# Where the squares and sums of three norms, the clearing of semaphores and the weight sums of split units stand in a two-block layer kernel

## The reference

```
def rms_norm(x, w):
    y = xf * lax.rsqrt(jnp.mean(xf * xf, axis=-1, keepdims=True) + EPS)
    return (y * w.astype(F32)).astype(x.dtype)

def conv_ffn(h, w_up, conv_w, conv_b, w_down):
    u = causal_dwconv(h @ w_up, conv_w, conv_b)
    val, gt = jnp.split(u, 2, axis=-1)
    return (jax.nn.silu(gt) * val) @ w_down

x = x + hybrid_mixer(h, ...)          # ends in merged @ w_out
h = rms_norm(x, norm_ffn[l]);  x = x + conv_ffn(h, ...)
return rms_norm(x, norm_final)
```

## Time and profile before

| what | us |
|---|---|
| median of 3 runs | 3509.37 |
| the profiled execution | 3512.56 |
| its span, first to last instruction | 3510.7 |
| PE busy | 3206.5 (91%) |
| DVE busy | 1542.1 (44%) |
| POOL busy | 942.8 (27%) |
| ACT busy | 662.1 (19%) |

### The profile page before, as it was taken

How to read it: one execution, slowest core, us unless ns; L and a number is a source line. 1 busy time by engine, 2 the same in 40 slices (tenths; PEclk the granted TensorE clock), 3 DMA queues, 4 the chain that set the end, 5 groups by cost and what they waited for, 6 DMA issues and landing times. The chain is left out here.

```text
span 3510.7 us, 54025 instructions
## 1 busy us (share of the span) xinstructions
PE 3206.5 (91%) x22800; PEld 2145.7 (61%) x22800; DVE 1542.1 (44%) x2277; ACT 662.1 (19%) x1320; POOL 942.8 (27%) x646
## 2 busy tenths in 40 slices
PE   8998999998999798988899999999979986999998
PEld 6855856883888487647566544455758854444432
DVE  4744466225655367534788403532344334111112
ACT  2233131011111433211110001111343211000001
POOL 2201213110322345212699860000365410000000
PEclk9999999998999899999999998989999968999999
DMA  4211223220232000032345432122210013899996
GB/s 158 79 31 44 76 78 107 74 72 0 72 109 71 1 4 3 32 126 66 108 126 155 153 118 65 56 78 61 84 38 3 3 48 127 310 407 409 409 409 253
DMA packets 120558, 406.09 MB, mean 116 GB/s; under 512 B 13824, under 2 KB 18560, under 8 KB 120064
## 3 DMA queue, kind: packets, MB, share of 16 engines
q1 hardware_dynamic: 113408, 377.47, 30.7%
q0 software_dynamic: 6912, 25.17, 2.3%
HBM read 398.39 MB, written 4.19 MB: 115 GB/s over the span
## 5 line engine op out<-in xcount | busy, mean ns | idle before, releaser
L701 PE MATMUL ps<-arena 128*128 128x256 f32 x4312 | 953.1, 384 | 42.6 <-DVE arena L644 12.6
L701 PEld LDWEIGHTS ps<-arena 128*128 128x128 f32 x4312 | 828.0, 192 | 174.0 <-issue 42.7
L428 PE MATMUL ps<-arena 128*128 128x512 f32 (+2 forms) x992 | 412.3, 575 | 34.7 <-PEq L657 14.2
L428 PEld LDWEIGHTS ps<-arena 128*128 128x128 f32 (+1 forms) x992 | 190.7, 195 | 251.6 <-issue 233.6
L3306 PE MATMUL ps<-arena 128*64 128x512 f32 x1024 | 239.3, 602 | 5.1 <-PE ps L3336 2.7
L734 PE MATMUL ps<-arena 128*128 128x512 f32 x496 | 224.6, 612 | 17.2 <-DVE arena L998 17.2
L632 POOL TENSOR_TENSOR arena<-arena 128x512 f32<-128x512 f32 x66 | 93.2, 1412 | 422.9 <-POOLq L1568 104.7
L3452 POOL TENSOR_SCALAR arena<-arena,small 128x1024 f32<-128x1024 f32 x64 | 189.5, 2961 | 10.2 <-DMA arena<-in_w_mod 6.4
L811 ACT ACTIVATE arena<-ps 128x256 f32<-128x256 f32 x231 | 86.5, 383 | 550.3 <-PE ps L701 543.1
L2289 POOL TENSOR_SCALAR arena<-arena,small 128x768 f32<-128x768 f32 x32 | 70.2, 2206 | 445.2 <-DVE small L2269 445.2
L734 PEld LDWEIGHTS ps<-arena 128*128 128x128 f32 x496 | 97.3, 197 | 138.7 <-issue 133.7
(11 more groups left out here) (438 smaller groups left out, 4423.7 us busy)
## 6 DMA issues: line engine op xcount, KB each, us to landing
arena<-in_w_in SPq DMA_DIRECT2D x166, 512.0 KB, 3.7
arena<-in_w_gate SPq DMA_DIRECT2D x128, 512.0 KB, 10.9
arena<-in_w_up SPq DMA_DIRECT2D x128, 512.0 KB, 15.0
arena<-in_w_down SPq DMA_DIRECT2D x128, 512.0 KB, 9.0
arena<-in_w_mod POOLq DMA_DIRECT2D x48, 512.0 KB, 4.3
arena<-in_ffn_up SPq DMA_DIRECT2D x44, 512.0 KB, 3.8
arena<-in_w_branch SPq DMA_DIRECT2D x32, 512.0 KB, 3.7
arena<-in_w_out SPq DMA_DIRECT2D x16, 512.0 KB, 4.1
```

The lines of the kernel that those rows point to most:

```text
L428: last = nc.tensor.matmul(out[0:m, 0:j["n"]], w[:, q * m:(q + 1) * m], j["rhs"](ka + q), start=(ka + n == 0), stop=(ka + n == kt - 1))
L701: last = nc.tensor.matmul(k.bank(b)[:, 0:HT], lhs[:, q * P:(q + 1) * P], rhs[:, q, :], start=(first and q == 0), stop=(q == 3), skip_group ...
```

## The change

1. Clearing. `recycle` and its block are gone. `retire` sets the old semaphores aside, POOL clears them at the end of its list in the following output projection (`afterwards`), and `reuse_retired` gives their numbers back after it. There are two such places instead of three: the first block's output projection, and the second block's, which takes the semaphores of both former places around the delta rule.
2. Norms. `ffn_norm`, the first block's last norm and the router's norm get `early=True`. Their squares and ones-products are issued inside the projection before (`tail`): ACT squares a plane after its eviction, PE adds it after a later unit or job, and the rest behind the last unit. At the old place the inversion, root and multiplication remain. The final norm's sums stand between the last pair's scatters, which use four banks.
3. Weight sums. DVE's sums of an S unit now stand in the *unit* before it, C or S, instead of the S unit before it; where the first unit is a C, only the turn stands at the start. POOL's order becomes join of u, S1 of the next, S3 of the next.
4. Orders. The LRU projection runs its convolved tiles first and its gelu tiles last; the feed-forward up stage's last group becomes four C units, so it has ten S units; the turned inputs of the second output projection lie in other planes. (`side` in `fast_phase` has no caller in this program.)

```diff
-    def recycle(self):
-        if self.phases and self.used:
-            with self.nc.Block() as block:
-                @block.gpsimd
-                def _(pool):
-                    for s in self.used:
-                        pool.sem_clear(s)
-            self.phases.close()
+    def retire(self):
+        self.old = self.phases, self.used
         self.phases, self.used = self.ctx.enter_context(ExitStack()), []
+    def clear_retired(self, pool):
+        for s in self.old[1]:
+            pool.sem_clear(s)
+    def reuse_retired(self):
+        self.old[0].close()
...
@@ project_phase, tensor
+                if tail is not None and i >= 1:
+                    tail.add(pe, i - 1)
+            if tail is not None:
+                tail.add(pe, len(jobs) - 1)
...
@@ fast_phase, gpsimd
                     later = splits[u["s"] + 1] if u["s"] + 1 < ns else None
+                    join(pool, nc.gpsimd, u)
                     if later:
                         sum_op(pool, nc.gpsimd, later, "S1", k.st_sump)
-                    join(pool, nc.gpsimd, u)
-                    if later:
                         sum_op(pool, nc.gpsimd, later, "S3", k.st_sump)
+            if afterwards is not None:
+                afterwards(pool)
@@ fast_phase, tensor
             for ui, u in enumerate(units):
+                if tail is not None and ui >= 2:
+                    while added < units[ui - 1]["i"]:
+                        tail.add(pe, added)
+                        added += 1
...
+            if tail is not None:
+                for c in range(added, KT):
+                    tail.add(pe, c)
@@ fast_phase, scalar, at the end of finish()
+                elif tail is not None:
+                    act.wait_ge(*j["evac"])
+                    tail.square(act, i)
@@ fast_phase, vector
-            sums_early(splits[0])
-            sums_late(splits[0])
-            for u in units:
+            if units.index(splits[0]) <= 2:
+                started.add(0)
+                turn(0)
+            if units[0] is splits[0]:
+                sums_early(splits[0])
+                sums_late(splits[0])
+            for ui, u in enumerate(units):
+                later = units[ui + 1] if ui + 1 < len(units) and units[ui + 1]["kind"] == "S" else None
                 if u["kind"] == "C":
+                    if later:
+                        sums_early(later)
+                        sums_late(later)
                     finish(u, 0)
                     continue
-                later = splits[u["s"] + 1] if u["s"] + 1 < ns else None
@@ class Norm
     def act(self, act):
-        for c in range(KT):
-            self.src_in(act, c)
-            nc.scalar.activation(self.sq(c), self.src(c), ACT.Square).then_inc(self.squared, 1)
+        for c in range(0 if self.early else KT):
+            self.square(act, c)
...
     def pe(self, pe):
+        for c in range(0 if self.early else KT):
+            self.add(pe, c)
@@ experts_phase
+    sum_bank = lambda u, c: (4, 5, 0, 1)[c % 4] if u == PAIRS - 1 else 4 + c % 2
-                if c >= 2 or u >= 1:
-                    pe.wait_ge(sc_out, 8 * u + max(c - 1, 0))
+                back = 4 if u == PAIRS - 1 else 2
+                if c >= back or u >= 1:
+                    pe.wait_ge(sc_out, 8 * u + max(c - back + 1, 0))
                     for c in range(8):
                         scatter(p - 2, c)
+                        if c >= 3:
+                            norm.add(pe, c - 3)
-            norm.pe(pe)
+            for c in range(5, KT):
+                norm.add(pe, c)
@@ order
-        plan(k, project_phase, k, tiles(W_LG, 8, g, func=ACT.Gelu_apprx_tanh)
-                      + convs(W_LX, 8, xc, "lru_conv_w", "lru_conv_b", 4, nch=8),
+        plan(k, project_phase, k, convs(W_LX, 8, xc, "lru_conv_w", "lru_conv_b", 4, nch=8)
+                      + tiles(W_LG, 8, g, func=ACT.Gelu_apprx_tanh),
...
-        up = Halves(k, [u for i in range(0, 44, 4) for u in (("C", i), ("C", i + 1), ("S", i + 2, 0))], ...
+        up = Halves(k, [u for i in range(0, 40, 4) for u in (("C", i), ("C", i + 1), ("S", i + 2, 0))] + [("C", i) for i in range(40, 44)], ...
```

More of the change, by code:

```diff
@@ L322, in wtile, with project_phase @@
     return [(w[i, :, a * P:min(a + 8, kt) * P], a, min(8, kt - a)) for a in range(0, kt, 8)]
[L325 removed]
+def project_phase(k, jobs, following=(), beside=None, moves=(), ahead=None, side=None, halves=None, afterwards=None, tail=None):
     if halves is not None:
[L334 removed]
+        return fast_phase(k, jobs, halves, following, beside, moves, ahead, afterwards, tail, side)
     nc = k.nc
@@ L538, in sum_plane, with fast_phase @@
         return self.k.pl(self.sums[(4 * s + n) % len(self.sums)])
-def fast_phase(k, jobs, h, following=(), beside=None, moves=(), ahead=None):
+def fast_phase(k, jobs, h, following=(), beside=None, moves=(), ahead=None, afterwards=None, tail=None, side=None):
     nc = k.nc
@@ L576, in fast_phase @@
             j["needs_n"] = jobs[j["needs"]]["post_n"]
+    if side is not None:
+        side.begin(jobs, moved, 16 * len(moves))
     free = [(b, None) for b in range(6)]
@@ L825, in _ @@
                     finish(u, 0)
+                if side is not None:
+                    for n in range(len(js)):
+                        side.act(act, u["i"] + n)
             if late is not None:
@@ L919, in _ @@
                     sums_early(later)
+                if side is not None:
+                    side.dve(dve, u["i"] + 1)
                 dve.wait_ge(*closing(u, "P3"))
@@ L973, in act, with square, add @@
         nc = self.k.nc
-        for c in range(KT):
-            self.src_in(act, c)
-            nc.scalar.activation(self.sq(c), self.src(c), ACT.Square).then_inc(self.squared, 1)
+        for c in range(0 if self.early else KT):
+            self.square(act, c)
         act.wait_ge(self.inverse, self.base + 1)
         nc.scalar.activation(self.rt, self.inv, ACT.Sqrt).then_inc(self.root, 1)
+    def square(self, act, c):
+        self.src_in(act, c)
+        self.k.nc.scalar.activation(self.sq(c), self.src(c), ACT.Square).then_inc(self.squared, 1)
+    def add(self, pe, c):
+        pe.wait_ge(self.squared, self.base * KT + c + 1)
+        ins = self.k.nc.tensor.matmul(self.sums, self.k.const("ones"), self.sq(c), start=(c == 0), stop=(c == KT - 1), skip_group_check=True)
+        if c == KT - 1:
+            ins.then_inc(self.summed, 1)
     def src_in(self, eng, c):
@@ L983, in pe @@
     def pe(self, pe):
-        for c in range(KT):
-            pe.wait_ge(self.squared, self.base * KT + c + 1)
-            last = self.k.nc.tensor.matmul(self.sums, self.k.const("ones"), self.sq(c), start=(c == 0), stop=(c == KT - 1))
-        last.then_inc(self.summed, 1)
+        for c in range(0 if self.early else KT):
+            self.add(pe, c)
     def dve(self, dve):
@@ L3593, in order @@
                                                     [WORK + 40 + n for n in range(9)]), moves=[(pl(X + c), dr["x"][c * P:(c + 1) * P, :]) for c in range(KT)])
-        plan(k, k.recycle)
+        plan(k, k.retire)
+        ffn_norm = NormThenSilu(k, lambda c: pl(X + c), H, lambda c: k.col("norm_ffn", c), WORK + 8, early=True)
         plan(k, project_phase, k, [job(wtile(dr["w_out"], c), lambda q: pl(MRG_PL + q), "D", pl(X + c), add=pl(X + c)) for c in range(KT)],
-             halves=halved(paired(8), [MRG_PL], [WORK + 16], [WORK + 24 + n for n in range(9)]))
+             halves=halved(paired(8), [MRG_PL], [WORK + 16], [WORK + 24 + n for n in range(9)]), afterwards=k.clear_retired, tail=ffn_norm)
+        plan(k, k.reuse_retired)
         if stage == "mixed":
@@ L3611, in order, with second_block @@
                               mul=pl(hid + i), needs=len(js) - 2))
-        up = Halves(k, [u for i in range(0, 44, 4) for u in (("C", i), ("C", i + 1), ("S", i + 2, 0))], [dict(x=H_PL, t=WORK + 8)], [MRG_PL + 4 + n for n in range(4)] + [WORK + 59], [WORK + 60, WORK + 61],
+        up = Halves(k, [u for i in range(0, 40, 4) for u in (("C", i), ("C", i + 1), ("S", i + 2, 0))] + [("C", i) for i in range(40, 44)], [dict(x=H_PL, t=WORK + 8)], [MRG_PL + 4 + n for n in range(4)] + [WORK + 59], [WORK + 60, WORK + 61],
                     [WORK + 16, WORK + 17], pool=False)
         plan(k, project_phase, k, js, beside=mod_products(k, acc, range(0, 4), 2), ahead=ffn_norm, halves=up)
+        last_norm = Norm(k, lambda c: pl(X + c), lambda c: pl(X + c), lambda c: k.col("norm_final", c), WORK + 8, early=True)
         plan(k, project_phase, k, [job(wtile(dr["ffn_down"], c, FT), lambda q: pl(hid + q), "D", pl(X + c), add=pl(X + c)) for c in range(KT)],
-             beside=mod_products(k, acc, range(4, 6), 4))
-        second_block(k, dr, out, stage, X, dump, acc)
-def second_block(k, dr, out, stage, X, dump, acc):
+             beside=mod_products(k, acc, range(4, 6), 4), tail=last_norm)
+        second_block(k, dr, out, stage, X, dump, acc, last_norm)
```

(1 more changed line is left out.)

34 lines of the change are left out of this document (21 added, 13 removed).

## The result

The changed kernel takes 3490.06 us (median of 4 runs, 3482.91 to 3491.05); the kernel before, on the same chip, 3509.39 (4 runs, 3505.91 to 3510.61). The ratio is 0.9942, with a 95% interval of 0.9925 to 0.9959: 19 us faster, where 23.7 were forecast.

The account below looks back on a forecast made before the run. PE was taken to bound the kernel nearly everywhere, so gains lie in its gaps. 47.1 us gained less 23.4 lost gives 23.7 less: median 3509.4 to 3485.7 us; own range 3474 to 3499, overall 3466 to 3505.

Parts of the forecast that it names:

- Clears: Stages that only clear semaphores: clearing moves beside the output projections' last split units and is hidden; 7.65 + 4.65 us gained.
- ffn norm: First block's ffn norm: squares and ones-products move into the projection before, so PE's gap shrinks; 4.1 us gained.
- LRU: End of the LRU projection: with gelu tiles last, PE's 6.75 us tail becomes 1.8; 4.9 us gained.
- Retention: Retention projection, eight single tiles: PE's stall at 698 us goes with sums one unit ahead; 6.7 us gained.
- The two merges: Among seven stages beginning with a split unit: POOL's third sum follows the join, each wait losing 1.1 us.
- the up stage: Inside the feed-forward up stage: moved sums delay ACT's copies, PE stalls 2.7 us in nine periods; 23.4 us lost.
- The four sums: DVE's weight sums between two single tiles' evictions in the up stage: 1.04 us each in the mean, 3.9 together.
- the second product's wait: Up stage: PE's second product waits for the first sum, 17.3 instead of 15.5 us, inside the 2.7 us stall.
- Rival 1: Up stage: DVE's backlog shrinks as much as the sums cost, no new stall; 3462.3 us, chance 0.12.
- Rival 2: Up stage: two of four sums stand behind POOL instructions, stall 5.9 us a period; 3515 us, chance 0.10.
- Rival 3: POOL's new order costs 0.3 us in each of 66 split units, 20 us in all; 3505.5 us, chance 0.09.
- Rival 4: Experts' stage: weight transfers, not PE, set its end, losing the router's 6.8 us and adding 2.7; 3495 us, chance 0.09.

Follow-up runs that it names:

- the experiment on the filled stall: Kernel before, plus seven unread ones-matrix products where PE stands still for 6.66 us in the retention projection: 3506.83 us, ratio 0.9986.
- the experiment on the filled second product: Changed kernel, plus three unread ones-matrix products ahead of PE's wait for the first sum in five up-stage split units: 3483.72 us, one run.

## Why the prediction was right, and where its terms were off

The mechanism was right on both sides, and the net within 5 us. How close the net came is in part luck: the gains were forecast some 12 us too low and the loss 15 us too low, and the two errors cancelled.

*Gains, forecast and profile.* Clears, ffn norm and the first unit behind them, from the start of the clearing stage to C0: 7.65 + 4.1 + 1.1 = 12.9 forecast, 77.4 - 64.8 = 12.6 found. Inside it the norm was over-priced: the 8.83 of the earlier trace rows was a slow start (granted clock 0.88 from 1670 to 1684), and in the run with the norms back at their heads, where it is 1.00 (1631 to 1645), the same eight products take 7.13 behind the same wait of 2.98, so the early norm gives 2.1. Second clearing 4.65, 4.7 found. Router 6.8, 6.7. Last norm 0.8, 1.4. Final norm 1.1, 1.0. Up stage's tail 3.7, 3.7. These hold.

*What was mis-sized: the edges where PE had waited long.* LRU 4.9 + 1.1 forecast, 9.3 found: 6.5 in the stage and 2.8 in the next one, whose products began at full clock (experiment: 4.9 + 2.0 by the order alone). Retention 6.7 + 1.1 forecast, 12.4 found: the two gaps, and 3.5 of PE's busy time (160.5 to 157.0). The two merges behind which I priced 1.1 each gave 3.3 each: 1.6 of gap and 1.7 of busy time. I counted a gap at its length; the rows show that the products behind it had been slow too. The granted clock of 0.57 and 1.00 in the experiment on the filled stall is that in a row. All gains together are some 59 us in the profile, not 47. Against them stand 39 us of the up stage (38.3, and 1.1 in its first period); the 2 us that remain to the difference of 22.0 lie in stages that vary between executions of one kernel (the first projection 177 to 180, the one with the `in_lora_g` loads 14 to 18).

*What was mis-sized: the up stage, 23.4 forecast, 38.3 found.* Step by step: nine periods by 2.7 are 24.3. PE needs the copy at 20.6, not 20.8: + 1.8. C0 is reached after 13.87 instead of 14.0: - 1.2. The copies start 5.24 after it, not 5.2: + 0.4. The four sums take 4.62 instead of 3.9: + 6.5. One period is early by 1.9, which a mean lets count against the others but a queue does not: + 1.9. That is the lateness of 33.7. The last 6 I read as products at the lower clock behind waits, which the experiment on the filled second product shows for one pair of units; with the 1.8 of before off, 38.3. So two steps were mis-sized. One is the four sums, priced at 3.9 a period and measured at 4.62. The other is the second product's wait, of which the forecast said that it "lies inside the 2.7 and doesn't add to it": it does not add by its length, but where it is 3 us long the products behind it are slow. And the mean of the earlier trace rows is one phase's mean; at another phase of POOL the four sums took 3.9, and the lateness was 26.7.

*The rivals.* Rival 1, no new stall, fell (40.1). Rival 2, the sums meet POOL, was half right: they do meet, but the sums took 4.6, not 7.1, and the stall was 4.5 a period, under the 5.2 at which the change would have lost. By the rule of the Trainium skill ("SBUF — State Buffer", section "SBUF: two separate sides") a sum would wait until the end of the POOL instruction that it meets. The timeline above agrees for one kind and not for the other. The sum at 1689.54 began 0.14 into POOL's two-input instruction and took 2.84, ending 0.55 after it. The sum at 1688.94, far into POOL's one-input instruction of 3.16, took 0.68; the one at 1693.01, 0.24 into the next such, took 1.49, though that ran to 1695.69. From the second period to the stage's end it is the same: of 24 two-input DVE instructions that began inside POOL's two-input one, 23 ended 0.55 behind its end. Of the 49 that began inside its one-input one, the 38 that began more than 1.4 us into it took their undisturbed 0.68 to 0.75, and of the 11 earlier ones nine took 1.5 to 1.6 and ended 1.19 before its end. Here the measurement decides: a one-input instruction of POOL held DVE only at its beginning. Rival 3, POOL's order costs in the steady state, fell with the experiment on it: 12 us faster. Rival 4 fell: the experts' stage is 520.5 against 521.4.

*Not settled.* Why POOL's one-input instruction lets DVE in after about a microsecond no run here isolates. The lateness at each phase was measured, not predicted; a forecast good to 2 us would have to run the two queues against each other from the first instruction. The split between clock and phase of what filling the second product's wait gained is shown for one unit pair only. Each stall is read from one profiled execution of its version, and the experiments with POOL's work shifted, with the sums behind C1, with the second product's wait filled and with the LRU order back have a single run each; whether the phase differs between executions of one kernel is open. What made the eight ones-products of the earlier trace rows start slowly in before and not in the run with the norms back is open too, as the wait ahead of them is the same 2.98.

## What to carry to other kernels

Work moved out of an engine's own waiting time and into the space between two evictions can cost its length once for each period, even where the engine's total is the same; with POOL's work cut and 3.3 us of slack behind it, the same place cost nothing. Ask who stands behind it in the other engines' queues, and with how much slack. Price a vanished gap on PE at its length plus what the granted-clock row shows of the products behind it. And when a change touches many places, test the one place that loses by itself: here it took back two thirds of what the others gained.

## What the runs showed of the hardware that I had not expected

- PE, DVE and ACT with the same work lose 31 or 40 us in a stage according to POOL's phase: more work on POOL (three clearings) made the stage 8 us shorter, and taking back a good edit hid 10 us of its own loss.
- DVE instructions over 512 columns with a PSUM source kept 0.75 and 0.81 us in the up stage of every variant; those with two SBUF inputs ranged from 0.68 to 2.84, and the two convolution taps from SBUF took 0.75 without POOL and 1.38 and 1.12 in the mean beside it.
- A clear of a semaphore costs POOL 0.044 us of its own and 0.071 from one to the next, 188 of them 13.3 us; two blocks for them alone cost PE 14.0.
